# A third pair of chunks in seven block products: output chunks 2 and 3 of a hybrid attention layer

## What is computed

```python
h = rmsnorm(x, g_norm)
proj = jnp.einsum('bsd,de->bse', h, w_in)          # 256 x 2048 times 2048 x (15 chunks of 512)
...
y_moba = rmsnorm(o_moba * jax.nn.silu(m_z), g_out_moba)
y_nsa = rmsnorm(o_nsa * jax.nn.silu(n_z), g_out_nsa)
y = jnp.concatenate([y_moba, y_nsa], axis=-1)      # 256 x 2048
x = x + jnp.einsum('bse,ed->bsd', y, w_out)        # 256 x 2048 times 2048 x 2048
return rmsnorm(x, g_final)
```

## Time and profile before

| | |
|---|---|
| median of 3 runs | 498.32 us (498.15 to 498.80) |
| the profiled execution, its own time | 498.54 us |
| its span in the profile | 496.7 us |
| PE busy | 487.2 us (98%) |
| DVE busy | 335.6 us (68%) |
| ACT busy | 250.5 us (50%) |
| POOL busy | 60.9 us (12%) |

### The profile page before, as it was taken

How to read it: one execution, slowest core, us unless ns; L and a number is a source line. 1 busy time by engine, 2 the same in 40 slices (tenths; PEclk the granted TensorE clock), 3 DMA queues, 4 the chain that set the end, 5 groups by cost and what they waited for, 6 DMA issues and landing times.

```text
span 496.7 us, 6459 instructions
## 1 busy us (share of the span) xinstructions
PE 487.2 (98%) x2512; PEld 405.4 (82%) x2512; DVE 335.6 (68%) x535; ACT 250.5 (50%) x358; POOL 60.9 (12%) x66
## 2 busy tenths in 40 slices
PE   8999999999999999999999999999999999999993
PEld 7888788787788888888888888888888888888882
DVE  5887544345879948766587878666888766765442
ACT  5884335353556535544544464665664544545421
POOL 2340101000102202000020200000323131022020
PEclk9999999999999999999999999999999999999998
DMA  8989788585353452443443734346257577367222
GB/s 293 332 286 378 247 292 307 201 287 179 133 198 136 170 170 85 170 154 105 166 168 129 254 100 146 138 169 255 84 170 290 218 248 242 103 254 252 86 85 85
DMA packets 54543, 96.45 MB, mean 194 GB/s; under 512 B 4368, under 2 KB 13168, under 8 KB 54128
## 3 DMA queue, kind: packets, MB, share of 16 engines
q1 hardware_dynamic: 54480, 96.03, 55.5%
q10 hardware_dynamic: 32, 0.01, 0.0%
HBM read 93.93 MB, written 2.10 MB: 193 GB/s over the span
## 4 chain that ended last, share of the span: by engine, by line
PE 95%; issue 2%; DMA 1%; DVE 0%; ACT 0%; ACTq 0%; POOLq 0%; POOL 0%; DVEq 0%
PE proj L647 26%; PE proj L649 25%; PE proj L648 25%; PE b_o L941 4%; PE b_t L628 2%; PE b_p L910 2%; PE b_s L810 2%; PE proj L680 2%; PE proj L686 1%; PE proj L691 1%; DMA xo<-in_x_dram 1%; PE b_s L649 1%; PE b_s L647 1%; PE b_s L648 1%; PE b_p L628 0%
## 5 line engine op out<-in xcount | busy, mean ns | idle before, releaser
L1341 DVE TENSOR_TENSOR w_lo<-w_raw,w_hi 128x2048 fp32r<-128x2048 f32 x68 | 157.5, 2319 | 87.6 <-ACT w_hi L1018 87.4
L647 PE MATMUL proj<-w_hi,xT_hi 128*128 128x512 f32 x484 | 191.0, 395 | 0.0
L649 PE MATMUL proj<-w_hi,xT_lo 128*128 128x512 f32 x484 | 188.8, 390 | 0.0
L648 PE MATMUL proj<-w_lo,xT_hi 128*128 128x512 f32 x484 | 188.6, 390 | 0.0
L1018 ACT ACTIVATE w_hi<-w_raw 128x2048 fp32r<-128x2048 f32 x68 | 129.7, 1911 | 34.9 <-PE proj L649 24.5
L647 PEld LDWEIGHTS proj<-w_hi,xT_hi 128*128 128x128 f32 x484 | 90.9, 188 | 20.1 <-issue 1.6
L649 PEld LDWEIGHTS proj<-w_hi,xT_lo 128*128 128x128 f32 x484 | 90.9, 188 | 19.4
L648 PEld LDWEIGHTS proj<-w_lo,xT_hi 128*128 128x128 f32 x484 | 91.0, 188 | 17.8
L1155 ACT ACTIVATE pT<-b_p 128x512 f32<-128x512 f32 (+2 forms) x24 | 11.7, 489 | 53.9 <-PE b_p L910 53.9
L595 POOL TENSOR_TENSOR rope_a<-rope_a,rope_b 128x512 f32<-128x512 f32 (+1 forms) x12 | 13.1, 1109 | 160.8 <-DVE rope_b L1428 160.8
L647 PE MATMUL proj<-w_hi,ymT_hi 128*128 128x512 f32 x80 | 31.2, 390 | 0.0
(11 more groups left out here) (249 smaller groups left out, 555.5 us busy)
## 6 DMA issues: line engine op xcount, KB each, us to landing
w_raw<-in_w_in_dram SPq DMA_DIRECT2D x53, 1024.0 KB, 4.9
w_raw<-in_w_out_dram SPq DMA_DIRECT2D x16, 1024.0 KB, 5.1
xo<-in_w_ck_dram SPq DMA_DIRECT2D x4, 1024.0 KB, 7.8
xo<-in_w_cv_dram SPq DMA_DIRECT2D x4, 1024.0 KB, 7.8
w_raw<-in_w_in_dram SPq DMA_DIRECT2D x12, 256.0 KB, 6.8
Q<-in_x_dram SPq DMA_DIRECT2D x1, 2048.0 KB, 9.8
out_dram<-Q SPq DMA_DIRECT2D x8, 256.0 KB, 2.9
xo<-in_x_dram SPq DMA_DIRECT2D x3, 512.0 KB, 7.9
```

Source lines behind the costliest of these rows:

```text
L647: nc.tensor.matmul(dst, a_hi, b_hi, start=first, stop=False, skip_group_check=goes_on)
L648: nc.tensor.matmul(dst, a_hi, b_lo, start=False, stop=False, skip_group_check=goes_on)
L649: return nc.tensor.matmul(dst, a_lo, b_hi, start=False, stop=last, skip_group_check=goes_on)
L1341: nc.vector.tensor_tensor(wl, w_raw[:, u % RAW], wh.bitcast(F32), ALU.subtract).then_inc(lo_ready, 1)
```

## The change

Output chunks 2 and 3 become pair number 2. Their first units, (2,0) and (3,0), are no longer loaded and multiplied; seven block products on four blocks of `w_out` and on sums of the first four k tiles of y take their place. The rest of the chunks is still plain: (3,1), (2,1), (2,2), (2,3), (3,2), (3,3) are units 64, 65, 66, 67, 68, 69. A pair's slots stand in tables now.

```diff
-OUT_UNITS = [(0, 0), (0, 1), (1, 0), (1, 1), (0, 2), (1, 2), (0, 3), (1, 3)] + [(c, g) for c in (2, 3) for g in range(4)]
-OUT_DONE = [NPROJ + max(i for i, u in enumerate(OUT_UNITS) if u[0] == c) for c in range(3)]
-PAIRS = [(11, 12, 44), (13, 14, 52)]
+OUT_UNITS = [(0, 0), (0, 1), (1, 0), (1, 1), (0, 2), (1, 2), (0, 3), (1, 3)]
+OUT_DONE = [66, 67, 72]
+PAIRS = [(11, 12), (13, 14), (NC + 2, NC + 3)]
+FIRST_BLOCKS, T2_SLOT, EARLY, LATE_BLOCKS = [40, 48, 66], [41, 49, 67], [42, 50, 68], [43, 51, 69]
+MIDDLE, LATE = [44, 52, 69], [45, 53, 70]
...
+    a, b = PAIRS[2]
+    ring.append(("early", 2))
+    plain(b, 1)
+    ring.append(("middle", 2))
+    plain(a, 1)
+    ring.append(("late", 2))
+    for c, g in ((a, 2), (a, 3), (b, 2), (b, 3)):
+        plain(c, g)
...
-    return ROUNDED_AT.get(slot) if slot < 60 else slot - 2
-OUT_SLOT = OUT_DONE[:2] + [OUT_DONE[2] + 2]
+    return slot - 2 if 60 <= slot < 66 else ROUNDED_AT.get(slot)
+OUT_SLOT = OUT_DONE[:2] + [OUT_DONE[2] + 1]
...
-                if u == 50:
-                    sp.wait_ge(blk_lo, 7)
+                if u in (50, 62):
+                    p = (50, 62).index(u) + 1
+                    sp.wait_ge(blk_lo, 7 * p)
                     for n in range(4):
-                        block(1, n)
+                        block(p, n)
...
-                if g == 0:
+                opens = g == 0 or (c, g) == (PAIRS[2][1], 1)
+                if opens:
                     bank_free(c)
...
             def last_chunk():
-                bank_free(NC + 3)
                 for m in range(MT):
-                    for g in range(UPC):
+                    for u in (NU - 2, NU - 1):
...
+            def ys_round():
+                act.wait_ge(xs_ok, 2)
+                act.wait_ge(unit_used, used_by_chunk(NC - 1))
+                nc.scalar.activation(ys_hi, ys, ACT.Copy).then_inc(xs_hi_ok, 1)
...
+                if slot == 65:
+                    ys_round()
...
+            def mid_add(i):
+                m, c = ((0, 3), (1, 2), (0, 2), (1, 3))[i]
+                dve.wait_ge(mid_out, 4 * 2 + i + 1)
+                a = acc[:, m, c * CW:(c + 1) * CW]
+                nc.vector.tensor_tensor(a, mid_copy(2, i), a, ALU.add).then_inc(mid_added, 1)
+
+            def y_sums():
+                dve.wait_ge(ylo_done, 2)
+                dve.wait_ge(y_done, 8)
...
+                step(nc.vector.tensor_tensor(ys, ymT_hi[:, 0:UK, :].bitcast(F32), ymT_lo[:, 0:UK, :].bitcast(F32), ALU.add), 5)
+                step(nc.vector.tensor_tensor(d, c, d, ALU.add), 6)
+                step(nc.vector.tensor_tensor(c, a, c, ALU.subtract), 7)
+                step(nc.vector.tensor_tensor(a, d, a, ALU.subtract), 8)
+                nc.vector.tensor_tensor(b, b, a, ALU.subtract).then_inc(xs_ok, 1)
+
+            def ys_residual():
+                dve.wait_ge(xs_hi_ok, 2)
+                nc.vector.tensor_tensor(ys_lo, ys, ys_hi.bitcast(F32), ALU.subtract).then_inc(xs_lo_ok, 1)
...
+                if slot == 65:
+                    ys_residual()
...
+                if slot == 64:
+                    y_sums()
```

More of the change, by code:

```diff
@@ L78, in stream @@
     plain(first - 1, 3)
-    for p, (a, b, _) in enumerate(PAIRS):
+    for p, (a, b) in enumerate(PAIRS[:Z_PAIRS]):
         ring.append(("middle", p))
@@ L713, in unit @@
                     for k in range(UK):
-                        last = three_products(*operands(u, m, k), g == 0 and k == 0, g == UPC - 1 and k == UK - 1, c in PAIR_OF)
+                        last = three_products(*operands(u, m, k), opens and k == 0, k == UK - 1 and (g == UPC - 1 or c in PAIR_OF), c in PAIR_OF and not opens)
                 last.then_inc(unit_used, 1)
@@ L727, in seven @@
                 pe.wait_ge(blk_lo, 7 * p + n + 1)
-                xh, xl = [t[:, k0:k0 + 2, m * P:(m + 1) * P] for t in (xT_hi, xT_lo)] if of == "x" else                          [t[:, m, k0:k0 + 2, :] for t in (xs_hi, xs_lo)]
+                if of == "s" and p < Z_PAIRS:
+                    xh, xl = [t[:, m, k0:k0 + 2, :] for t in (xs_hi, xs_lo)]
+                else:
+                    pair = (ys_hi, ys_lo) if of == "s" else (xT_hi, xT_lo) if p < Z_PAIRS else (ymT_hi, ymT_lo)
+                    xh, xl = [t[:, k0:k0 + 2, m * P:(m + 1) * P] for t in pair]
+                if p == 2 and bank_no >= 2:
+                    new = False
                 wh, wl = block_split(p, n)
@@ L1089, in mid_out_ @@
                     act.wait_ge(t_round, len(ROUNDS))
-                if p and i == 0:
+                if p == 1 and i == 0:
                     act.wait_ge(pv_done, 2 * NH)
-                if p and i in (1, 2):
+                if p == 1 and i in (1, 2):
                     act.wait_ge(y_done, 2)
+                if p == 2:
+                    act.wait_ge(y_done, 8)
+                    nc.scalar.activation(mid_copy(p, i), mid_bank(p, i)[:, :], ACT.Copy).then_inc(mid_out, 1)
+                    return
                 m = (0, 1, 0, 1)[i]
@@ L1290, in _ @@
                     prob_out(JOB_AT[slot - 2])
-                for p in range(len(PAIRS)):
-                    if slot == PAIRS[p][2] - 1:
-                        block_hi(p, 4)
-                        block_hi(p, 5)
+                if slot in LATE_BLOCKS[:Z_PAIRS]:
+                    for n in (4, 5):
+                        block_hi(LATE_BLOCKS.index(slot), n)
                 if slot % UPC == UPC - 1 and slot < NPROJ and ACT_READS[KINDS[slot // UPC]]:
@@ L1695, in _ @@
                         block_lo(p, 1)
-                    if slot == s0 - 2 and p:
+                    if slot == EARLY[p] and p:
                         block_lo(p, 2)
@@ L1699, in _ @@
                         t3(p)
[L1700 removed]
+                    if slot == LATE[p]:
                         block_lo(p, 6)
[L1702 to L1703 removed]
+                        if p == 1:
+                            z_times(PAIRS[0][1])
+                if slot == LATE_BLOCKS[2]:
+                    block_lo(2, 4)
+                    block_lo(2, 5)
                 if slot > 1 and rounded_at(slot) is not None and rounded_at(slot) < NU:
                     lo(rounded_at(slot))
[L1706 removed]
+                if slot == EARLY[0]:
                     block_lo(0, 2)
                     block_lo(0, 3)
[L1709 removed]
+                if slot == LATE_BLOCKS[0]:
                     t3(0)
                     t4(0)
[L1712 to L1714 removed]
+                if slot in T2_SLOT:
+                    t2(T2_SLOT.index(slot))
+                if slot == EARLY[2]:
+                    t4(2)
+                if slot == 64:
+                    y_sums()
+                for i, at in enumerate((69, 69, 70, 71)):
+                    if slot == at:
+                        mid_add(i)
                 if slot == 2:
@@ L1743, in _ @@
                     row_max(JOB_AT[slot])
-                for p in range(len(PAIRS)):
-                    if slot == PAIRS[p][2] - 1:
-                        block_lo(p, 4)
-                        block_lo(p, 5)
+                if slot in LATE_BLOCKS[:Z_PAIRS]:
+                    for n in (4, 5):
+                        block_lo(LATE_BLOCKS.index(slot), n)
                 if slot % UPC == UPC - 1 and slot < NPROJ and KINDS[slot // UPC] == "z":
```

85 lines of the change are left out of this document (47 added, 38 removed).

## The result

| | before | after |
|---|---|---|
| median | 498.56 us (498.15 to 498.86, 4 runs) | 506.52 us (505.41 to 506.71, 4 runs) |
| ratio, after to before | | 1.0156, 95% interval 1.0138 to 1.0173 |
| profiled execution, its time | 498.54 us | 506.68 us |
| its span | 496.7 us | 504.9 us |

The change makes the kernel about 8 us, 1.6%, slower. I forecast 504.6 with a range of 503.0 to 508.0. The side and the range hold, but the 1.9 us between forecast and result belong to one of the rivals, the fall of PE's clock.

What follows compares the result with a forecast made beforehand. The prediction took the kernel as bound by PE's matmuls, with ACT and DVE hidden. -1.36 + 2.06 + 0.40 + 4.73 + 0.42 = +6.25 us on 498.32 gave 504.6 us, range 503.0 to 508.0.

Steps and rivals of the forecast that it cites:

- the fall of PE's clock: Rival: clock halves in the wait ahead of unit 64, twelve slow matmuls cost 2.7 us, time 507.3; chance 0.25.
- Six matmuls: On PE: 48 - 42 = 6 matmuls fewer at 0.227 us each, 1.36 us gained.
- First wait: Slot 67: PE waits for `lo(63)`, delayed by sums, round and residual, and starts unit 63 2.06 us late.
- Second wait: P1: PE waits for chunk 0's residuals to free its banks and starts at 447.52, 0.40 us late.
- Third wait: Unit 64: PE stands from 450.24 until chunk 1's residuals are done, starting at 454.97, 4.73 us of wait.
- The restart behind a semaphore: PE's start again behind a wait: taken as 0.27 us, a weight load of 0.19 and 0.08 for the semaphore.
- a part of the chain is hidden: Rival: ACT and DVE delays hold PE up only in part, time 499 to 503.5; chance 0.12.
- Fourth wait: Unit 65 in `pair_middle`: POOL's products hold up DVE's block 2, so PE starts 0.42 us late.
- the full clock: Case taken as likeliest: the waits as walked without a clock fall, 503.5 to 505.4; chance 0.57.
- The gain arrives: Rival: PE never waits, time 497.0, deciding at a chain through ACT and DVE shorter by 5.8 us; chance 0.03.

Runs made afterwards that it cites:

- sums_early: Changed kernel with the sums of y moved from slot 64 to 60, their rounding to slot 61, their residual behind `lo(62)`: 500.10 us, ratio 1.004.
- hi64_first: Changed kernel with `hi(64)` on ACT moved ahead of the squares of output chunk 0, nothing else: 503.63 us, ratio 1.0098 to the kernel before.
- both: Changed kernel with the moves of sums_early and hi64_first together, no matmul filled in: 497.33 us, ratio 0.9978 to the kernel before.
- fill_all: Changed kernel with identity matmuls nobody reads, 7 ahead of unit 63 and 18 ahead of unit 64: 503.73 us, ratio 1.0108.
- fill: Changed kernel with eight identity matmuls nobody reads put on PE ahead of unit 64: 505.39 us, ratio 1.0141 to the kernel before.
- sums_early_fill: The sums_early kernel with eight identity matmuls nobody reads in its wait ahead of unit 64: 499.08 us, ratio 1.0015 to the kernel before.

## Why the prediction came out as it did

**Six matmuls, -1.36: right.** PE's count is 2506, six fewer than the 2512 before, and where nothing waits 1.47 us come out.

**First wait, +2.06: right** to 0.14. `lo(63)` was forecast at 439.12 and came at 439.10; PE started at 441.54, forecast 441.68: 0.15 behind `lo(63)` and not 0.27. sums_early takes the sums away and the wait is gone.

**Second wait, P1 at 447.52: right.** It came at 447.32, with 0.2 us of it lost to DVE's residuals instead of 0.40: the restart took 0.10 and not 0.27.

**Third wait, unit 64 at 454.97: right.** It came at 454.92. Each link was within 0.04 us: `hi(64)` 448.10 (448.13), `lo(64)` 450.03 (450.06), the residuals 453.38 (453.41). The restart behind a semaphore, estimated at 0.27, was 0.26 here, the only place where the sum needed it. That is luck in part: it was 0.15 and 0.10 at the other two waits, and at none did a weight load of 0.19 stand ahead of the matmul, as the estimate had it; in the records the first load starts 0.03 to 0.04 ahead of it (454.88 and 454.92). That the chain is one and its early part shifts all the rest is shown by sums_early and hi64_first, which shorten it at different places, and by both, which takes off nearly all of it. The rival that a part of the chain is hidden falls.

**Fourth wait, +0.42: mis-sized.** Block 2 was held, 1.89 us instead of 1.23, which is 0.66 where I had taken 0.87. Block 3 and `t3` followed 1.13 behind the start of the one before, not 1.15. At the full clock the wait is 0.1 us (fill_all), and in the changed kernel the slow unit 64 covers it.

**"I take 504.6", the full clock: this step failed.** The rival with chance 0.25 is what happened. The range holds because it was made wide enough for that rival; the case that I took, 503.5 to 505.4, did not come. The rival's 2.7 us for twelve slow matmuls is near the 2.85 of the profile and the 2.8 of fill_all, but twelve was a choice and not worked out: about fourteen were slow, at 0.20 us more for each and not 0.227. In the sum 1.9 us are missing from the forecast: +2.85 for the clock, -0.42 for the fourth wait, -0.43 for the tail, which I had left as it was without a reason, -0.05 for the third. I had weighed it too low because I held one fall, at 3.2 us of idleness, against a doubt, though the third wait, at 4.7, was longer than the one idle stretch of which the rows told the outcome. And in the expectations I was wrong to hold waits of about 2 us to be free of it: the profiles of fill and hi64_first show falls behind 1.8 us, and the times and mean clocks of sums_early point to falls behind 2.3 us.

**The gain arrives: it can.** It was to decide at a chain shorter by 5.8 us. sums_early takes off 4.84 (454.92 to 450.08) and is still slower; both takes off 6.62 and is faster.

**What stays open.** Why one execution of the same kernel keeps the clock behind a wait of 2 us and the next one doesn't is not to be read from these profiles, since only one of each is recorded. For the same reason it is open where the slower executions of fill and hi64_first lost their time. Nor is where the 0.43 us of the tail come from.

## What to carry to other kernels

A kernel at 95% PE still has a hidden chain behind it. Before work is saved on PE, walk the lists of the helping engines in order with durations from the trace: here that gave the start of unit 64 to 0.05 us, and it showed that new work for DVE and ACT stood ahead of the roundings that PE waits for next. If such work is there, move it to where its inputs are ready and the engines are idle: the same change with the sums four slots sooner and one rounding ahead of two squares is 0.2% faster, and with POOL's products out of the way 0.35%, instead of 1.6% slower. A wait of PE cost its length here and then up to 2.9 us of slow matmuls. Where the wait can't be removed, matmuls without a result can keep the clock up: in fill_all and sums_early_fill, where they took up most of every long wait, the scatter went; in fill, where they took up less than half of one and none of the other, it stayed.

## What the runs showed of the hardware

**The clock can fall after PE is back at work.** In fill PE stood for 1.8 us, up to 441.52, and the clock fell near 442.6, 1.1 us after the restart; it was 0.51 over 444 to 446 and full from there. In the changed kernel, behind 4.6 us, it was 0.50 from 454.0 to 460.0 and full again from 461.0. The first wait of 1.8 us left it full in that execution and not in those of fill and hi64_first. In hi64_first it fell 0.5 us after the restart.

**DVE and POOL hold each other up, both ways.** `t2` (two inputs in SBUF, 1024 elements) took 2.31 us against 1.22 alone, and POOL's two products took 5.28 against 2.54, when they met. The rows of both fit whole operations in turn. POOL's first product starts at 442.72, inside `lo(64)` (442.34 to 444.62), and ends at 445.76, 1.27 after 444.49. `t2` starts at 444.54 and ends at 446.85, 1.22 after 445.63, where POOL's first product is about to end. POOL's second starts at 445.73 and ends at 448.00, 1.27 after 446.73, where `t2` is about to end. Chunk 1's residuals, which read one input from PSUM, ran beside that second product from 446.77 on and took their usual 1.28.
The Trainium skill, "SBUF — State Buffer", section "Who interferes with whom", has one lock for the two, held for a whole instruction; the rows agree.
